# Weaving two mixer units of a transformer block into a triangular inversion

## The reference, cut to what matters

```python
for l in range(2):
    x = layer_norm(ALPHA * x + swiglu_half(x, ffn1_w1[l], ffn1_w3[l], ffn1_w2[l]), ...)
    a_u, a_v, b_qkv, b_z, b_beta, b_decay, c_q, c_k, c_v, c_r, c_g = split(x @ w_in[l])
    out_a = spatial_gating(gelu(a_u), gelu(a_v), ...)        # u * (tril(w_s) @ layer_norm(v) + b_s), chunks of 128
    out_b = gated_deltanet(b_qkv, b_z, b_beta, b_decay, ...) # 8 heads of 64: solve (I + L) u = rhs, then a recurrence
    out_c = gla(c_q, c_k, c_v, c_r, c_g, ...)                # 4 heads, chunks of 64: linear attention with decay
    mix = concatenate([out_a, out_b, out_c]) @ w_out[l]
    x = layer_norm(ALPHA * x + mix, ...)
    x = layer_norm(ALPHA * x + swiglu_half(x, ffn2_w1[l], ffn2_w3[l], ffn2_w2[l]), ...)

# gla, per head and chunk c of 64 tokens, a = decay of each key channel
S_next = exp(bcum_last) * S + k_dec.T @ v                    # the state
o      = o_intra + q_dec @ S
```

## Time and profile before

| | |
|---|---|
| three runs | 4484.00, 4482.46, 4483.39 us, median 4483.39 |
| the profiled execution | 4480.93 us, its span from first to last instruction 4478.7 us |
| busy | TensorE 89%, VectorE 50%, GpSimd 29%, ScalarE 18% of the span |
| mean granted clock of TensorE | 0.920 |
| gating, linear attention and its norm, first and second layer | 92.56 and 93.58 us |
| chain that ended last | TensorE 57%, VectorE 8%, ScalarE 3%, issue 1% of the span |

### The profile page before, as it was taken

How to read it: one execution, slowest core, us unless ns; L and a number is a source line. 1 busy time by engine, 2 the same in 40 slices (tenths; PEclk the granted TensorE clock), 3 DMA queues, 4 the chain that set the end, 5 groups by cost and what they waited for, 6 DMA issues and landing times.

```text
span 4478.7 us, 45446 instructions
## 1 busy us (share of the span) xinstructions
PE 3972.2 (89%) x18934; PEld 3231.3 (72%) x18934; DVE 2246.4 (50%) x3669; ACT 793.7 (18%) x1470; POOL 1284.0 (29%) x522
## 2 busy tenths in 40 slices
PE   7976888999997899999999647999999997658998
PEld 5964468999984578888878425788788785346886
DVE  4734557876644452343455264634633472457334
ACT  3024332101124320100011221100100121311001
POOL 1310002333330044444444000444344341003443
PEclk9989899999998999999999657999999997569999
DMA  5400002343320022232222000222222221002222
GB/s 195 151 29 1 1 15 88 124 127 125 106 71 10 19 87 97 97 109 99 96 84 98 19 0 15 84 95 99 87 94 99 90 92 45 0 1 71 99 94 85
DMA packets 103695, 335.61 MB, mean 75 GB/s; under 512 B 11426, under 2 KB 11586, under 8 KB 103236
## 3 DMA queue, kind: packets, MB, share of 16 engines
q1 hardware_dynamic: 78192, 282.29, 18.8%
q10 hardware_dynamic: 25300, 50.43, 3.6%
HBM read 330.58 MB, written 2.10 MB: 74 GB/s over the span
## 4 chain that ended last, share of the span: by engine, by line
PE 57%; DVE 8%; ACT 3%; issue 1%; DVEq 0%; ACTq 0%
PE PS L497 48%; PE PS L979 1%; DVE XH L778 1%; PE PS L890 1%; PE PS L1835 1%; DVE arena L1935 0%; DVE arena L1933 0%; PE PS L499 0%; PE PS L1595 0%; PE PS L1596 0%; DVE H_r L655 0%; PE PS L1701 0%; DVEq L319 0%; PE PS L1838 0%; PE PS L970 0%
## 5 line engine op out<-in xcount | busy, mean ns | idle before, releaser
L497 PE MATMUL PS<-arena_r,ring_hi 128*128 128x512 f32 (+1 forms) x6272 | 2118.1, 376 | 98.2 <-DVE H_r L655 94.8
L2164 POOL TENSOR_TENSOR ring_r<-ring,ring_hi 128x1024 fp32r<-128x1024 f32 x518 | 1283.8, 2480 | 3159.7 <-DVE ring_hi L337 3159.7
L497 PE MATMUL PS<-arena_r,ring_r 128*128 128x512 f32 (+1 forms) x4800 | 1799.7, 375 | 0.0
L497 PEld LDWEIGHTS PS<-arena_r,ring_hi 128*128 128x128 f32 x6272 | 1177.4, 189 | 282.4 <-issue 99.1
L497 PE MATMUL PS<-H_r,ring_hi 128*128 128x512 f32 (+1 forms) x3328 | 1249.4, 375 | 0.0
L497 PEld LDWEIGHTS PS<-arena_r,ring_r 128*128 128x128 f32 x4800 | 906.7, 189 | 133.5
L497 PEld LDWEIGHTS PS<-H_r,ring_hi 128*128 128x128 f32 x3328 | 632.0, 190 | 93.8 <-issue 0.5
L337 DVE CAST ring_hi<-ring 128x1024 fp32r<-128x1024 f32 x518 | 503.3, 974 | 277.9 <-DMA ring<-weights_dram 277.3
L1482 DVE SCALAR_TENSOR_TENSOR arena<-arena,PS 128x512 f32<-128x512 f32 x88 | 60.5, 688 | 449.1 <-PE PS L497 449.1
L1478 ACT ACTIVATE arena<-PS 128x512 f32<-128x512 f32 x88 | 52.6, 598 | 1073.1 <-PE PS L497 1073.1
L1093 DVE SCALAR_TENSOR_TENSOR XH<-PS,mods,XH 128x256 f32<-128x256 f32 (+1 forms) x144 | 68.5, 523 | 208.5 <-PE PS L497 208.5
(11 more groups left out here) (340 smaller groups left out, 3456.9 us busy)
## 6 DMA issues: line engine op xcount, KB each, us to landing
ring<-weights_dram SPq DMA_DIRECT2D x534, 512.0 KB, 3.3
rstd<-ada_later_dram ACTq DMA_DIRECT2D x54, 256.0 KB, 2.7
mean<-ada_later_dram ACTq DMA_DIRECT2D x53, 256.0 KB, 2.8
ada_extra<-ada_later_dram ACTq DMA_DIRECT2D x53, 256.0 KB, 2.9
XH<-xT_dram ACTq DMA_DIRECT2D x1, 3072.0 KB, 22.9
out_dram<-XH SPq DMA_DIRECT2D x8, 256.0 KB, 2.0
con<-second_dram ACTq DMA_DIRECT2D x1, 1536.0 KB
con<-first_dram ACTq DMA_DIRECT2D x1, 1280.0 KB, 8.1
```

Of the source, the lines that this page charges most:

```text
L497: ins = pe.matmul(PS[:, o.bank, 0:hi - lo], w[:, 0, :], x, **flags)
L2164: nc.gpsimd.tensor_tensor(ring_lo[:, slot, :, :], ring[:, slot, :, :], ring_hi[:, slot, :, :].bitcast(F32), ALU.subtract).then_inc(lo_read ...
```

## The change

The gating unit's and the linear attention's stages are gone as stages of their own. `solve_*` is divided: `form_*` builds the triangular blocks, and behind a new barrier comes one stage that inverts them and does both units. On VectorE their operations stand between the transposes and between the row steps of the inversion; on TensorE and ScalarE they stand before the inversion's own. `gla_norm` is joined with `gdn_norm` to `mix_norm` of six items. The state of the linear attention is updated by one scalar_tensor_tensor per chunk, after the updates of all chunks were masked by four operations. Buffers move so that nothing overlaps: the masked weights behind the constants, the small rows in `scratch` and `ada_extra`, XD in `silu_ctx`, others in places that q, k and v of the delta rule have left. Two small loads move from before the feed-forward product to before the input product.

```diff
-        GS = (0, 1, 6, 7)
+        GS = (4, 5, 2, 3)
+        UPDATE_BANKS = ((6, 7), (2, 3))
...
+        def units_pe(pe, l):
+            pe.wait_ge(small_loaded.sem, 64 + 48 * l)
+            pe.matmul(PS[:, 4, :], gup[0:16, :], gl[0:16, :], start=True, stop=True).then_inc(ga_low.sem, 1)
             for t in range(2):
                 ins = pe.matmul(PS[:, 0, :], C("ones"), vp_[:, t, :], start=(t == 0), stop=(t == 1))
             ins.then_inc(sg_z.sem, 1)
...
             ins.then_inc(sg_t.sem, 1)
+            pe.wait_ge(ga_prod.sem, ga_prod.next("pe"))
+            for n in range(NLT):
+                ins = pe.transpose(PS[:, 5, P * n:P * n + P], kdec[:, P * n:P * n + P], C("ident"))
+            ins.then_inc(ga_kt.sem, 1)
             pe.wait_ge(sg_tc.sem, sg_tc.next("pe"))
+            pe.wait_ge(ga_ktc.sem, ga_ktc.next("pe"))
+            for c in range(7):
+                o, n = 64 * (c % 2), c // 2
+                ins = pe.matmul(update_bank(c), kdt[o:o + 64, n, :], vg[o:o + 64, n, :], start=True, stop=True)
+            ins.then_inc(ga_st.sem, 1)
             pe.wait_ge(sg_w.sem, sg_w.next("pe"))
             for h in range(4):
...
             ins.then_inc(sg_z.sem, 1)
+            pe.wait_ge(ga_state.sem, ga_state.next("pe"))
+            for h in range(4):
...
+                ins.then_inc(ga_s.sem, 1)
+            pe.wait_ge(ga_pt.sem, ga_pt.next("pe", 4))
...
+            ins.then_inc(ga_o.sem, 1)
...
+        def gla_states_dve(dve):
             dve.wait_ge(ga_st.sem, ga_st.next("dve"))
-            for c in range(7):
-
-                nc.vector.tensor_scalar(Sg[:, c + 1, :], Sg[:, c, :], gtg[:, c:c + 1], None, ALU.mult)
-                v_link(dve, nc.vector.tensor_tensor(blocks, update_bank(c), C("bd_gla", 0, 256), ALU.mult))
-                v_link(dve, nc.vector.tensor_tensor(Sg[:, c + 1, :], Sg[:, c + 1, :], blocks, ALU.add))
+            for odd in range(2):
+                for b in range(2):
+                    cs_ = [c for c in range(odd, 7, 2) if c // 4 == b]
+                    ins = nc.vector.tensor_tensor(Sg[:, cs_[0] + 1:cs_[-1] + 2:2, :],
+                                                  PS[:, UPDATE_BANKS[odd][b], 0:256 * len(cs_)].rearrange("p (a b) -> p a b", a=len(cs_)),
+                                                  C("bd_gla", 0, 256).unsqueeze(1).to_broadcast([P, len(cs_), 256]), ALU.mult)
+            v_link(dve, ins)
+            for c in range(1, 7):
+                ins = nc.vector.scalar_tensor_tensor(out=Sg[:, c + 1, :], in0=Sg[:, c, :], scalar=gtg[:, c:c + 1], in1=Sg[:, c + 1, :],
+                                                     op0=ALU.mult, op1=ALU.add)
+                if c < 6:
+                    v_link(dve, ins)
+            ins.then_inc(ga_state.sem, 1)
...
-        def solve_dve(dve):
-            nc.vector.memset(X64[quad(0), :, 32:64], 0.0)
+        def form_dve(dve):
...
+        def solve_dve(dve, l):
+            def blocks_in(q):
+                return nc.vector.transpose(LD[quad(q), :, :], lt_blocks(q))
+            blocks_in(0)
+            blocks_in(1)
+            centre_v_dve(dve)
+            blocks_in(2)
+            gla_decay_dve(dve)
+            v_link(dve, blocks_in(3))
+            mask_w_dve(dve, l)
+            norm_v_dve(dve, l)
+            gla_products_dve(dve)
+            rows_dve_of_inverse(dve, 0, 10)
+            gla_states_dve(dve)
+            rows_dve_of_inverse(dve, 10, 24)
+            sgu_out_dve(dve)
+            gla_mask_dve(dve)
+            rows_dve_of_inverse(dve, 24, 31)
             for q in range(4):
-                if q < 3:
-                    nc.vector.transpose(X64[quad(q), :, 32 * (q % 2):32 * (q % 2) + 32].rearrange("p m c -> p c m"),
-                                        XD[quad(q), :, :].rearrange("p i c -> p c i"))
-                ins = nc.vector.transpose(lt_blocks(q), XD[quad(q), :, :])
+                nc.vector.transpose(lt_blocks(q), XD[quad(q), :, :])
+            gla_out_dve(dve)
+            nc.vector.memset(X64[quad(0), :, 32:64], 0.0)
+            for q in range(3):
+                ins = nc.vector.transpose(X64[quad(q), :, 32 * (q % 2):32 * (q % 2) + 32].rearrange("p m c -> p c m"),
+                                          XD[quad(q), :, :].rearrange("p i c -> p c i"))
             ins.then_inc(so_x.sem, 1)
...
-            add_gemm(in_plan(l))
-            add(sgu_pe, sgu_act, lambda e, l=l: sgu_dve(e, l))
-            add(lambda e, l=l: gla_pe(e, l), lambda e, l=l: gla_act(e, l), lambda e, l=l: gla_dve(e, l))
-            add(*gla_norm[l])
+            add_gemm(in_plan(l), before=third_loads(l))
             add(*l2_qk)
             add(lambda e, l=l: rows_pe(e, l), lambda e, l=l: rows_act(e, l), lambda e, l=l: rows_dve(e, l))
-            add(solve_pe, solve_act, solve_dve)
+            add(form_pe, form_act, form_dve)
+            add(lambda e, l=l: (units_pe(e, l), solve_pe(e)), lambda e, l=l: (units_act(e, l), solve_act(e)), lambda e, l=l: solve_dve(e, l))
             add(rec_pe, rec_act, rec_dve)
-            add(*gdn_norm[l])
+            add(*mix_norm[l])
```

187 lines of the change are left out of this document (89 added, 98 removed).

## The result

The changed kernel takes 4356.9 us (median of four runs, 4353.8 to 4358.2) against 4482.9 us for the kernel before, timed beside it: ratio 0.9718, 95% interval 0.9705 to 0.9730. The prediction was 4360 us. The profiled execution took 4357.44 us with a span of 4355.6 us and a mean granted clock of 0.934 (0.920 before).

The account below looks back on a forecast made before the run. Bound: a chain hopping between engines with barriers in the removed stages, VectorE alone in the inversion. -186.1 + 2 x 28.6 + 2 x 5.4 - 2 x 2.65 = -123.4 us, giving 4360 us; range 4343 to 4380.

Parts of the forecast that it names:

- What goes: The gating stage, linear-attention stage and its norm leave the path: 92.56 us in the first layer, 93.58 in the second.
- The layout of the woven stage: Merged inversion stage: 73.3 us from barrier to first 32-wide matmul, +28.6 a layer; total 4350 to 4371 us, chance 0.71.
- The state operation: Linear-attention state update on VectorE: six 128x256 scalar_tensor_tensor, 0.46 us each with link, 2.8 us; bounds 0.42 and 0.69.
- TensorE at 1.2 GHz throughout: In the woven stage TensorE stays at its lower clock all through; the spatial products take 19.84 us.
- the first rival: Clock rises inside the woven stage, VectorE's waits shrink towards 0: up to 7.1 us a layer, 4346 us; chance 0.11.
- The rule weighed there: Sustained matmuls open the clock gate to 2.4 GHz, so the spatial products would take half of their 19.84 us.
- The q/k norm: Moved behind the dense product, its matmuls run at high clock: -2.65 us a layer, bounds 0 and 2.65.
- The joined norm: Two more items in the norm: +2.8 us on VectorE, +2.6 on ScalarE before it, +5.4 a layer.
- Nothing for the rest: Moved small loads, the new barrier (0.1 us), the forming stage's memset, recurrence and feed-forward leave the time unchanged.
- a leaking weave: Late handoff in woven stage holds VectorE's queued row steps: 5 to 15 us a layer, 4372 to 4390; chance 0.13.
- nothing is hidden: Both units take their old 82 us a layer inside the new stage; gain 10.8 a layer, 4462 us; chance 0.03.
- The dense products lost no clock: Rival: dense products lose granted clock after shorter idle stretches; slower below 0.963, about 4495 us; chance 0.02.

Follow-up runs that it names:

- Keys late: Changed kernel with ScalarE copying the turned keys seven times instead of once, so TensorE idles before the state updates: 4363.85 us, ratio 0.9735.
- the wide bias: Changed kernel with the spatial bias added by one matmul of 512 columns per head instead of four of 128: 4354.35 us, ratio 0.9711.
- the pause: Changed kernel plus a stage of 14 linked ScalarE copies between the input product and the q/k norm of each layer: 4377.34 us, ratio 0.9763.
- the unwoven kernel: Changed kernel with the same single stage, but VectorE does all operations of both units before the inversion: 4431.63 us, ratio 0.9885.

## Why the prediction was right

By its own steps:

- *What goes* held: both stages and their norm are off the path.
- *The layout of the woven stage* held in order and, in layer 1, nearly in size. The 32-wide blocks start 71.85 us behind the barrier there, 73.3 predicted. VectorE's waits were 1.94, 0, 1.34, 1.64 and 0.80 against 1.9, 0.2, 1.2, 2.0 and 1.75. The 1.5 us between them: outputs 0.85 earlier behind the last mask than the earlier trace rows had them, because the change leaves out two of their products with the zero state (the first two groups of L1631 take 0.69 us each instead of 1.12), which the prediction overlooked; and the last three transposes in 5.72 us instead of 6.3, whose source XD now lies in another buffer than their target. In layer 2 the blocks start after 68.4 us, and the waits were 0.82, 0, 0, 0.66 and 0.79.
- *The state operation* cost 3.09 us for six, 0.50 each with its link, not 0.46; inside the bounds of 0.42 and 0.69. Folding it is worth 2.9 us a layer on a bare chain, and 2.6 to 3.4 in woven stages whose products begin at the high level.
- *TensorE at 1.2 GHz throughout* is the step that held only in part, and with it the first rival has a share of truth. In the earlier trace rows the products took 19.84 us, and they were at 0.50; the 0.53 that the prediction calls the lower level is the mean of a stretch whose first 6.4 us were at the high one. Of the sixteen woven stages in the eight traces of the changed kernel and its variants that keep these products and their place in the weave, four show that time (19.7 to 19.8 us); in the other twelve the clock is high for the first 3 to 5.5 us of them and they take 15.9 to 17.6. (Keys late, whose place is 3.8 us later, has one of each.) In the changed kernel that is the difference between +27.0 and +23.9 us a layer. So the price of 28.6 us a layer fits the rarer course of the clock, and that the first trace had it in one layer is luck. The rival's form, no waits at all, did not come: even the fastest stage of the changed kernel waited 2.3 us (mean, masks, outputs).
- *The rule weighed there*, the Trainium skill, "TensorE: Matmul & The Clock Gate", section "Part 1: The HAM clock gate", by which sustained matmuls open the gate: the trace disagrees for these blocks. They run without a pause, and wherever the clock was high as they began, or rose just behind that, it fell while they ran (3 to 5.5 us into them); only with the wide bias, where they are done in 8.2 us, did they end before it fell. The long dense stretches are at 1.00 (1600 to 2200 us), and there the trace agrees with the rule.
- *The q/k norm* gained 2.6 us a layer, as predicted, and the pause shows that the idle time before it is the cause.
- *The joined norm* cost 5.7 and 4.7 us for 5.4.
- *Nothing for the rest* missed 0.9 us a layer in the forming stage. VectorE's last wait for the keys' products is 3.97 us there and was 3.12 before; TensorE's matmuls ran at lower clock at that place. It is within the scatter: the same code takes 38.4 to 40.15 us in the traces of the changed kernel and its variants, and that of the kernel before 38.7 to 40.0 in its two.
- *The rivals*: a leaking weave is excluded by the waits, of which none was later than laid out by more than 0.14 us; that nothing is hidden, by the unwoven kernel, which also shows that this rival was overpriced: even unwoven the change gives 53 us, where it had 21. The dense products lost no clock, 0.96 and 1.00 in the same stretches of both traces.

That the sum came within 3 us owes something to chance: the layers gave 3.5 us more than laid out, and the unchanged part took 3.8 us more.

## What to carry to other kernels

Where one stage keeps a single engine busy and another is a chain between the others, lay the chain's handoffs on the clock of the busy engine and ask of each only whether it is early enough: here five waits, predicted from starts in the old timeline, came true within a microsecond each in the layer where the clock took the assumed course, and were up to 1.3 us shorter in the other. Merging two independent chains into one stage is worth much by itself (an estimated 12 to 15 us a layer here, from the 21 of the unwoven kernel without the folded states, the products left out and the clock), before any weaving into the busy engine's work (37 us). A saving on an engine is worth its length only where that engine sets the pace: the folded states gave their 2.9 us on the bare chain and 2.6 to 3.4 in the weave, and the copies moved off VectorE gave their 2.3 us a layer in both; the wide bias, which takes an estimated 3.1 us off TensorE at the low level, gave 0.9 us in one layer and nothing in the other. And where the clock's course differs from execution to execution by more than an edit is worth, compare stages of the same course; the medians had put the folding in the weave at 0.9 us a layer.

## What the runs showed of the hardware

- The granted clock within a stage changes from execution to execution of one program: the same 64 instructions took 19.73 us in one trace of the changed kernel and 17.36 in the other. Differences of 2 to 3 us between two traces of such a stage say nothing about an edit, unless the clock took the same course in both.
- Fourteen update instructions more, priced at 3.75 us at the lower level, took 1.7 and 2.0 us, and the medians show no cost; idle time of 3.8 us at the same place cost its whole length and in one layer the high clock as well. A doubled cost is therefore no sure test of a price on TensorE at low clock.
- With sixteen narrow bias matmuls among the spatial products the granted clock fell at the latest 5.5 us into them, though they run without a pause; with four wide ones it stayed high past their end in two stages, and low all through in two others.
- A 32x1024 transpose on VectorE took 2.17 us with source and target both in `arena` and 1.90 us with the source in `silu_ctx`.
- A scalar_tensor_tensor of 128x256 takes 0.48 us of busy time, 0.06 us more than the two-operand form of that size and well under the 0.69 of a form of 512 columns.
